# Wider updates of x, odd tiles scaled in PSUM, and a new load order in a hybrid mLSTM/SSD diffusion step

## The chip, the cores and the metric

The kernel runs on one core of a Trainium2 chip. Its time is device time in microseconds (us) of one execution; several runs are taken and the median counts. The engines named below are TensorE (PE; its weight loads are shown apart as PEld), VectorE (DVE), ScalarE (ACT), GpSimd (POOL) and SyncE (SP), which here only issues loads and stores. All data is fp32.

## The reference, cut to what matters

One trunk layer on 128 prompt tokens and 256 latent tokens, D = 2048: a SwiGLU half step, a token mixer, a second SwiGLU half step. Each is fed by a modulated norm and added to x through a second norm and a gate:

```python
mod = (silu(c) @ w_ada + b_ada).reshape(1, 9, D)          # shift, scale, gate for three stages
h = rmsnorm(x, g[0]) * (1 + scale) + shift
x = x + 0.5 * gate * rmsnorm(swiglu(h, w_gate, w_up, w_down), g[1])
h = rmsnorm(x, g[2]) * (1 + scale) + shift                # the same with the mixer's mod
proj = h @ w_in                                           # q, k, v, gates, z, xbc, dt
x = x + gate * rmsnorm(mix, g[3])
h = rmsnorm(x, g[4]) * (1 + scale) + shift
x = x + 0.5 * gate * rmsnorm(swiglu(h, ...), g[5])
```

The mixer runs a chunked mLSTM and a chunked Mamba-2 scan in both directions; its input xbc goes through a depthwise convolution of five taps and its gates through cumulative sums and maxima.

## The kernel before

Every large product is done as three fp32r products: weights and activations are split into a high part (ACT) and a low part (POOL for weights and even tiles, DVE for odd tiles), and PE adds hi x hi, lo x hi and hi x lo (`product`, L804 to L806; in the down projections L921 to L923).

**Pieces and the ring of loads.** A piece is 512 KB of weights in one of eight slots of `w_raw`. SP issues the loads in the order of the pieces (`load`, L700); a load waits until the piece eight places earlier has been used up: a main piece when POOL has made its low part (`make_lo`, L2526, three pieces ahead of PE), a modulation piece (w_ada) when PE has multiplied it (`ada_piece`, L835). PE uses the pieces in the order of the same list.

**Passages.** Between the stages x is updated and normed. There are two passages with a turn of x, after the first FFN and after the mixer, and an end after the second FFN. In `end_of` (L1913) DVE adds the last products to y, finds the root of y's mean square per token block c (0 the prompt, 1 and 2 the latents), and updates x in twelve pieces of 512 columns (`finish`, L1905). ACT squares the same pieces for the next norm (`square_block`, L1443), POOL multiplies y by the gate rows (`gain`, L2537). PE then turns x into 16 tiles of 128 features (`turn`, L885), spreads the roots of x over the partitions (`spread_root`, L896), and DVE scales each turned tile out of PSUM into one of four SBUF tiles (`scaled`, L1759). ACT adds the shift and rounds to the high part (`hi_of`, L1365), POOL (even tiles, L2531) and DVE (odd tiles, `odd_low`, L1773) make the low part. The first products of the next stage follow tile by tile, and each turns a tile four ahead. `HI_ORDER` and `LO_ORDER` say between which tiles ACT and POOL convert the next weight pieces. In `passage` (L1037) PE also runs matmuls of ones whose result nobody reads (`stay_awake`, L880); `WAKE` holds their numbers: 4, 8, 8 in the first passage, 24, 8, 8 in the second.

**The gate stage.** After the first passage PE runs 28 main pieces (gate columns and xbc of w_in) among 28 modulation pieces (the mod of the mixer's gate and some more). Call them m0 to m27 and a0 to a27. The order is a0 to a3, the passage, m0, m1, m2, a4, m3, a5 and so on: a(j) follows m(j-2). The loads have the same order. A group of modulation pieces ends in columns: DVE copies the sums out (`ada_rows_out`, L1796, the copy is L1801), PE turns them into columns (`ada_columns`, L868, the matmul is L876), DVE adds the bias (`ada_store`, L1841). The first group holds a0 to a15, then three groups of four. `MIX_COLUMNS` (L132) says after how many main pieces the columns of a group come. DVE works in order, and between these steps stand the convolutions (`conv`, L2170) and five parts of the gate arithmetic (`gate_part`, L2087). ACT stores the gain rows of the mixer in this stage (`store_gains`, L1437), element by element:

```python
act.dma_start(g_wait[stage, g].rearrange("(k p) -> p k", p=P), coefG[:, :, g], allow_slow_non_contiguous=True)
```

Of the kernel before, what the change touches and what calls it, by code (L numbers as in the profile page):

```python
# [188 lines left out]
WAKE = ((4, 8, 8), (24, 8, 8))  # L189
# [14 lines left out]
XS = [[("x", c, cc) for cc in range(4)] for c in range(3)]  # L204
YS = [("y", c, cc) for c, cc in ADD_ORDER[:6]]
SQUARES = (
    YS + [("y", 0, 2), ("y", 0, 3), ("y", 1, 2)] + XS[0] + [("y", 1, 3), ("y", 2, 2)] + XS[1][:2] + [("y", 2, 3)] + XS[1][2:] + XS[2],
    [("y", c, cc) for cc in (2, 0, 1) for c in range(3)] + [("y", 0, 3)] + XS[0] + [("y", 1, 3)] + XS[1][:2] + [("y", 2, 3)] + XS[1][2:] + XS[2],
    [("y", c, cc) for c, cc in ADD_ORDER],
)  # L210
# [127 lines left out]
def hybrid_step(nc, A):  # L338
    with ExitStack() as ctx:
# [75 lines left out]
        y_square = am(37, 2 * 512).rearrange("p (s n) -> p s n", s=2)  # L415
        y_gain = am(20.5, NCH * 2 * 512).rearrange("p (c b n) -> p c b n", c=NCH, b=2)
# [206 lines left out]
        GAIN_ORDER = [(c, cc) for c in range(NCH) for cc in (1, 2, 3)]  # L623
        GAIN_ORDER = GAIN_ORDER[:5] + [(2, 1)] + [block for block in GAIN_ORDER[5:] if block != (2, 1)]
# [10 lines left out]
        def square_at(stage, name, c, cc):  # L635

            return SQ_BASE[stage] + SQUARES[stage].index((name, c, cc))
# [9 lines left out]
        def wait_finished(eng, stage, c, cc):  # L647

            eng.wait_ge(x_fin, 12 * stage + 4 * c + cc + 1)
# [5 lines left out]
        def tok_block(c, cc):  # L655
            return y_tok[:, c, 512 * cc:512 * cc + 512]

        def x_block(c, cc):
            return x_tok[:, c, 512 * cc:512 * cc + 512]

        def gain_block(c, cc):
            return y_gain[:, c, cc - 2, :] if cc >= 2 else tok_block(c, cc)
# [8 lines left out]
        def g_block(stage, c, cc):  # L671
            return g_rows[stage][:, min(c, 1), 512 * cc:512 * cc + 512]

# [18 lines left out]
        FRESH_FIRST = GATE_FIRST + [FFN2, FFN2 + 1]  # L692
        assert all(p in M_OF for p in FRESH_FIRST)

        with nc.Block() as block:
# [3 lines left out]
            def _(sp):  # L699
# [88 lines left out]
                for n, (c, cc) in enumerate(OUT_BLOCKS):  # L788
                    sp.wait_ge(out_ready, n + 1)
                    dst = A["y_prompt"][0] if c == 0 else A["y_sample"][0, P * (c - 1):P * c]  # L790
                    sp.dma_start(dst[:, 512 * cc:512 * cc + 512], y_tok[:, c, 512 * cc:512 * cc + 512]).then_inc(out_stored, 16)

                sp.wait_ge(out_stored, 16 * NCH * (KT // 4))
# [6 lines left out]
            def _(pe):  # L800
# [79 lines left out]
                def stay_awake(n):  # L880

                    for _ in range(n):
                        pe.matmul(psum[7][:, 0:P], ones[:, :], ones[:, :], start=True, stop=True)

                def turn(stage, k):  # L885
# [151 lines left out]
                def passage(stage):  # L1037

                    stay_awake(WAKE[stage][0])
# [4 lines left out]
                    stay_awake(WAKE[stage][1])  # L1044
# [1701 lines left out]
```

## Time and profile before

| | |
|---|---|
| median of 3 runs | 3092.46 us (3089.41 to 3094.93) |
| profiled execution | 3091.71 us, span 3089.7 us |
| PE busy | 3009.0 us, 97% |
| POOL, DVE, ACT busy | 59%, 43%, 31% |
| DMA | 535.55 MB, mean 173 GB/s |

The span is what the hardware profiler saw between the first and the last instruction; the execution's own time has about 2 us more around it. Matmuls are pipelined, so PE's busy time is not PE at its peak. The granted clock is the share of full speed that PE was given: 1.00 is 2.4 GHz, 0.5 is 1.2 GHz.

### The profile page before, as it was taken

To read this page: it belongs to the slowest core of one execution; us is meant where nothing else is said; L and a number is where in the kernel's file an instruction comes from. 1 tells how busy PE (TensorE), PEld (TensorE's weight loads), DVE (VectorE), ACT (ScalarE), POOL (GpSimd) and SP (SyncE) were. 2 spreads that over 40 slices of the span, in tenths; PEclk is the share of its full clock that TensorE was granted. 3 is DMA by queue.
4 is the path that set the end of the run, shared out by engine and by line. 5 is a ranking of instruction groups with operands and counts; after the bars stand their busy time and mean duration, and the time that the engine had idled before them with its cause. 6 is when DMAs were issued, how large, how long until landed. Compare 5 with 4: busy or idle time off the path is not lost.

```text
span 3089.7 us, 46612 instructions
## 1 busy us (share of the span) xinstructions
PE 3009.0 (97%) x16689; PEld 2769.0 (90%) x16689; DVE 1331.2 (43%) x2849; ACT 971.5 (31%) x1259; POOL 1829.4 (59%) x908
## 2 busy tenths in 40 slices
PE   6999999999999998899999999899999999999998
PEld 2799999999999997789999988899999999999997
DVE  3365566556655665656743353523342111100113
ACT  2322322222223224424432233522222222222223
POOL 2565665565566665537865446566655666666666
PEclk8999999999999999999999999999999999999999
DMA  9866767666566664685444445236554654444343
GB/s 363 280 216 205 226 215 178 209 219 217 192 195 210 218 213 145 213 191 153 143 135 116 127 115 191 78 127 194 166 173 138 147 154 123 128 129 124 127 129 109
DMA packets 472242, 535.55 MB, mean 173 GB/s; under 512 B 37595, under 2 KB 401603, under 8 KB 470723
## 3 DMA queue, kind: packets, MB, share of 16 engines
q1 hardware_dynamic: 427904, 512.82, 53.1%
q10 hardware_dynamic: 44227, 21.30, 2.8%
q8 instruction: 64, 1.05, 0.1%
q14 instruction: 47, 0.39, 0.0%
HBM read 523.31 MB, written 9.69 MB: 173 GB/s over the span
## 4 chain that ended last, share of the span: by engine, by line
PE 77%; POOL 9%; issue 7%; DVE 4%; DMA 2%; ACT 1%; ACTq 1%; POOLq 0%; DVEq 0%; SPq 0%
PE banks L804 17%; PE banks L806 16%; PE banks L805 16%; PE banks L921 8%; PE banks L923 8%; PE banks L922 8%; POOL w_lo L2528 7%; DVE HB L2251 1%; DMA w_raw<-in_w_in_dram 1%; PE banks L835 1%; PE banks L1278 0%; PE banks L1298 0%; ACTq L1490 0%; DMA w_raw<-in_ffn_w_gate_dram 0%; PE banks L1283 0%
## 5 line engine op out<-in xcount | busy, mean ns | idle before, releaser
L2528 POOL TENSOR_TENSOR w_lo<-w_raw,w_hi 128x1024 fp32r<-128x1024 f32 (+1 forms) x668 | 1596.7, 2395 | 1035.0 <-ACT w_hi L1363 1034.5
L804 PE MATMUL banks<-xn_hi,w_hi 128*128 128x384 f32 x3664 | 1248.1, 341 | 13.9 <-POOL w_lo L2528 8.6
L805 PE MATMUL banks<-xn_lo,w_hi 128*128 128x384 f32 x3664 | 1229.0, 335 | 0.0
L806 PE MATMUL banks<-xn_hi,w_lo 128*128 128x384 f32 x3664 | 1228.9, 335 | 0.0
L1363 ACT ACTIVATE w_hi<-w_raw 128x1024 fp32r<-128x1024 f32 (+1 forms) x668 | 704.2, 1056 | 1514.3 <-PE banks L806 668.0
L804 PEld LDWEIGHTS banks<-xn_hi,w_hi 128*128 128x128 f32 x3664 | 691.2, 189 | 43.0 <-issue 26.7
L805 PEld LDWEIGHTS banks<-xn_lo,w_hi 128*128 128x128 f32 x3664 | 691.3, 189 | 4.2 <-issue 2.9
L806 PEld LDWEIGHTS banks<-xn_hi,w_lo 128*128 128x128 f32 x3664 | 691.0, 189 | 0.0
L1820 DVE SCALAR_TENSOR_TENSOR banks<-w_raw,cT,banks 128x256 f32<-128x256 f32 x1372 | 546.0, 482 | 0.0
L921 PE MATMUL banks<-w_hi,hid_hi 128*128 128x512 f32 x1056 | 411.9, 390 | 0.9 <-POOL w_lo L2528 0.9
L923 PE MATMUL banks<-w_lo,hid_hi 128*128 128x512 f32 x1056 | 411.3, 389 | 0.0
L922 PE MATMUL banks<-w_hi,hid_lo 128*128 128x512 f32 x1056 | 411.2, 389 | 0.0
L1974 DVE TENSOR_TENSOR y<-y,banks 128x512 f32<-128x512 f32 x252 | 158.2, 683 | 537.2 <-PE banks L923 537.0
L1985 DVE TENSOR_TENSOR AM<-AM,banks 128x384 f32<-128x384 f32 x88 | 44.8, 551 | 586.1 <-PE banks L806 586.1
L921 PEld LDWEIGHTS banks<-w_hi,hid_hi 128*128 128x128 f32 x1056 | 198.2, 188 | 42.7 <-POOL w_lo L2528 1.4
L923 PEld LDWEIGHTS banks<-w_lo,hid_hi 128*128 128x128 f32 x1056 | 198.2, 188 | 41.4
L922 PEld LDWEIGHTS banks<-w_hi,hid_lo 128*128 128x128 f32 x1056 | 198.2, 188 | 40.5
L2547 POOL TENSOR_TENSOR hid_lo<-AM,hid_hi 128x384 fp32r<-128x384 f32 x88 | 87.7, 1019 | 77.4 <-ACT hid_hi L1393 77.3
L1393 ACT ACTIVATE hid_hi<-AM 128x384 fp32r<-128x384 f32 x88 | 43.5, 525 | 164.9 <-DVE AM L1985 164.9
L2251 DVE SCALAR_TENSOR_TENSOR HB<-HB,AM,maskneg 128x128 f32<-128x128 f32 x96 | 83.3, 935 | 18.0 <-DMA HB<-row_wait 18.0
L835 PE MATMUL banks<-w_raw,cT 128*2 128x256 f32 x736 | 61.1, 432 | 18.1 <-DMA w_raw<-in_w_ada_dram 18.0
L1390 ACT ACTIVATE AM<-banks 128x384 f32<-128x384 f32 x88 | 38.4, 489 | 125.2 <-PE banks L806 125.1
(278 smaller groups left out, 1583.8 us busy)
## 6 DMA issues: line engine op xcount, KB each, us to landing
w_raw<-in_w_ada_dram SPq DMA_DIRECT2D x288, 512.0 KB, 5.6
w_raw<-in_ffn_w_gate_dram SPq DMA_DIRECT2D x176, 512.0 KB, 4.2
w_raw<-in_ffn_w_up_dram SPq DMA_DIRECT2D x176, 512.0 KB, 4.0
w_raw<-in_ffn_w_down_dram SPq DMA_DIRECT2D x176, 512.0 KB, 3.9
w_raw<-in_w_in_dram SPq DMA_DIRECT2D x104, 512.0 KB, 3.8
w_raw<-in_w_out_dram SPq DMA_DIRECT2D x32, 512.0 KB, 3.7
HB<-row_wait ACTq DMA_DIRECT2D x12, 512.0 KB, 4.4
AM<-g_wait SPq DMA_DIRECT2D x4, 1024.0 KB, 9.6
```

The costliest lines, as they stand in the source:

```text
L804: pe.matmul(out, wh, hi, start=start, stop=False)
L805: pe.matmul(out, wh, lo, start=False, stop=False)
L806: return pe.matmul(out, w_lo[:, w, off:off + P], hi, start=False, stop=stop)
L835: last = pe.matmul(ada_bank(unit)[32 * s:32 * s + 2, 0:PC], cT[:, n * q + s // h, :], w_raw[:, p % NR, s * PC:s * PC + PC], start=(q == 0) ...
L921: pe.matmul(bank[:, :], hi, wh, start=start, stop=False)
L922: pe.matmul(bank[:, :], lo, wh, start=False, stop=False)
L923: return pe.matmul(bank[:, :], hi, wl, start=False, stop=stop)
L1363: act.activation(used(w_hi[:, slot(p), :], p), used(w_raw[:, p % NR, :], p), ACT.Copy).then_inc(w_hi_ready, 1)
L1820: ins = dve.scalar_tensor_tensor(out=dst, in0=w, scalar=c, in1=acc, op0=ALU.mult, op1=ALU.add)
L1974: dve.tensor_tensor(tile, tile, psum[token_bank(cc, c)][:, :], ALU.add).then_inc(y_done, 1)
L2251: last = dve.scalar_tensor_tensor(out=seg[:, n % 2, h, :], in0=seg[:, n % 2, h, :], scalar=cols[:, C_Q, c, r0 + h:r0 + h + 1], in1=maskneg ...
L2528: pool.tensor_tensor(used(w_lo[:, slot(p), :], p), used(w_raw[:, p % NR, :], p), used(w_hi[:, slot(p), :], p).bitcast(F32), ALU.subtract). ...
```

## The change

- **Updates of x.** `finish`, `square_block` and the stores of the output take a width. x is updated in seven pieces, (c, first block, blocks): (0,0,2), (0,2,2), (1,0,2), (1,2,2), (2,0,2), (2,2,1), (2,3,1), in a new order of `end_of`. The order of POOL's gains changes with it.
- **Odd tiles.** An odd turned tile is scaled in place in its PSUM bank; ACT and `odd_low` read it there. Odd tiles take turns in two banks, and the turn of tile k waits for the low part of tile k-4.
- **Load order.** The loads of the gate stage get an order of their own: a(j) directly behind m(j), not behind m(j-2). PE's order (now `GATE_ORDER`, `GATE_EXEC`) stays, and counts of PE's events are renumbered to it.
- **Columns.** The first group's columns come after main piece 16 (m15) and not ahead of a16; the others after 21, 25 and 28 main pieces and not 19, 23 and 27.
- **Wake matmuls.** 8 ahead and 4 behind in the first passage, 16 and 4 in the second, none between the roots.
- **Weights between tiles.** In the second passage ACT and POOL convert the sixth and seventh weight piece of the FFN between tiles 12 and 15 and not behind the last tile.

```diff
-MIX_COLUMNS = {19 + 4 * k: ADA_PASS + k for k in range(ADA_MIX)}
+MIX_COLUMNS = {16: 0, 21: ADA_PASS, 25: ADA_PASS + 1, 28: ADA_PASS + 2}
-GATE_PIECES = [("a", 0, q) for q in range(PASS_PIECES)] + GATE_PIECES
+GATE_ORDER = [("a", 0, q) for q in range(PASS_PIECES)] + GATE_PIECES
+GATE_MAINS = [piece for piece in GATE_PIECES if piece[0] == "x"]
+GATE_PIECES = GATE_ORDER[:PASS_PIECES] + GATE_MAINS[:5]
+for k, piece in enumerate(MIX_ADA):
+    GATE_PIECES += [piece] + GATE_MAINS[5 + k:6 + k]
...
+for n, piece in enumerate(GATE_ORDER):
+    N_PE[P_GATES + GATE_PIECES.index(piece)] = N_PE[P_GATES - 1] + n + 1
+GATE_EXEC = [(P_GATES + GATE_PIECES.index(piece), *piece) for piece in GATE_ORDER]
...
-WAKE = ((4, 8, 8), (24, 8, 8))
+WAKE = ((8, 4), (16, 4))
...
+FINISHED = [(0, 0, 2), (0, 2, 2), (1, 0, 2), (1, 2, 2), (2, 0, 2), (2, 2, 1), (2, 3, 1)]
...
-TURN_BANKS = ((1, 4), (4, 6))
+TURN_BANKS = ((4, 1, 5), (4, 6, 7))
...
-            ((2, range(5)), (3, range(5, 8)), (4, range(8, 11)), (None, range(11, KT))))
+            ((2, range(5)), (3, range(5, 8)), (4, range(8, 11)), (5, range(11, 13)), (6, range(13, 15)), (None, (15,))))
...
-            ((1, (0, 2)), (2, (4,)), (3, (6,)), (4, (8, 10)), (None, (12, 14))))
+            ((1, (0, 2)), (2, (4,)), (3, (6,)), (4, (8, 10)), (5, (12,)), (6, (14,))))
...
-        FRESH_FIRST = GATE_FIRST + [FFN2, FFN2 + 1]
+        FRESH_FIRST = GATE_FIRST + [FFN2, FFN2 + 1, FFN2 + 2, FFN2 + 3]
...
                 def turn(stage, k):
-                    if k >= 2:
+                    if k % 2 == 0 and k >= 2:
                         pe.wait_ge(xt_done, KT * (stage + 1) + k - 1)
+                    if k == 3:
+                        pe.wait_ge(xt_done, KT * (stage + 1) + 1)
+                    if k % 2 and k >= 5:
+                        pe.wait_ge(xn_lo_odd, KT // 2 * (stage + 1) + (k - 5) // 2 + 1)
                     for c in range(NCH):
-                        last = pe.transpose(psum[TURN_BANKS[stage][k % 2]][:, P * c:P * c + P], x_tok[:, c, P * k:P * k + P], idn[:, :])
+                        last = pe.transpose(turn_bank(stage, k)[:, P * c:P * c + P], x_tok[:, c, P * k:P * k + P], idn[:, :])
...
                 def passage(stage):
-                    stay_awake(WAKE[stage][0])
+                    stay_awake(WAKE[stage][0], 7)
                     for k in range(2):
                         turn(stage, k)
                     for c in range(2):
                         spread_root(stage, c)
-                    stay_awake(WAKE[stage][1])
                     spread_root(stage, 2)
                     for k in range(2, TURN_AHEAD):
                         turn(stage, k)
-                    stay_awake(WAKE[stage][2])
+                    stay_awake(WAKE[stage][1], 0)
...
                 def scaled(stage, k):
-                    src = psum[TURN_BANKS[stage - 1][k % 2]] if stage else y[:, k, :]
+                    src = turn_bank(stage - 1, k)[:, 0:TOK] if stage else y[:, k, :]
+                    dst = src if stage and k % 2 else xt[:, k % 4, :]
...
                 def odd_low(stage, k):
+                    src = turn_bank(stage - 1, k)[:, 0:TOK] if stage else xt[:, k % 4, :]
...
                 def end_of(stage):
+                    mixer, output = stage == 1, stage == 2
+                    if mixer:
+                        for c in range(NCH):
+                            root_bias(stage, "y", c)
+                    else:
+                        add_last(stage, 0, 2)
+                    add_last(stage, 0, 3)
+                    if not mixer:
+                        root_bias(stage, "y", 0)
+                    inverse(stage, "y", 0)
+                    finish(stage, 0, 0, 2)
+                    if not mixer:
+                        add_last(stage, 1, 2)
+                    finish(stage, 0, 2, 2)
+                    add_last(stage, 1, 3)
+                    if not mixer:
+                        root_bias(stage, "y", 1)
+                    if not output:
+                        root_bias(stage, "x", 0)
+                    inverse(stage, "y", 1)
+                    finish(stage, 1, 0, 2)
+                    if not mixer:
+                        add_last(stage, 2, 2)
+                    finish(stage, 1, 2, 2)
+                    add_last(stage, 2, 3)
+                    if not mixer:
+                        root_bias(stage, "y", 2)
+                    if not output:
+                        root_bias(stage, "x", 1)
+                    inverse(stage, "y", 2)
+                    finish(stage, 2, 0, 2)
+                    if not output:
+                        diagonal(stage, 0)
+                        diagonal(stage, 1)
+                    finish(stage, 2, 2, 1)
+                    finish(stage, 2, 3, 1)
+                    if not output:
+                        root_row(stage, 0, 2)
+                        root_bias(stage, "x", 2)
+                        diagonal(stage, 2)
```

## Rows read from the trace of the kernel before

**Rows 1.** Page, part 1: engine, busy us (share of the span) and instructions.
```profile
PE 3009.0 (97%) x16689; PEld 2769.0 (90%) x16689; DVE 1331.2 (43%) x2849; ACT 971.5 (31%) x1259; POOL 1829.4 (59%) x908
```
**Rows 2.** Windows: start:end, length, then busy us per engine, granted clock, DMA share, GB/s.
```profile
core 0: us, PE busy (x) PEld busy (x) DVE busy (x) ACT busy (x) POOL busy (x), PEclk, DMA share, GB/s
...
1195.00:1260.00 65.00, 51.69 (x311) 43.98 (x310) 44.71 (x93) 38.52 (x97) 34.30 (x25) 0.89 0.35 110
...
1300.00:1360.00 60.00, 49.90 (x301) 43.10 (x300) 41.64 (x79) 13.91 (x20) 18.89 (x8) 0.89 0.74 139
...
1960.00:2000.00 40.00, 32.48 (x208) 30.79 (x207) 25.70 (x59) 26.96 (x58) 21.12 (x14) 0.97 0.17 53
```
**Rows 3.** Timeline of PE, gate stage: start, length, instruction, idle before and releaser.
```profile
1312.18 1.02 PE L876 MATMUL banks<-idn,ada_row 128*128 128x8 f32 x4 [6.52 <-DVE ada_row L1801]
...
1320.27 0.61 PE L835 MATMUL banks<-w_raw,cT 128*2 128x256 f32 x8
...
1325.18 0.61 PE L835 MATMUL banks<-w_raw,cT 128*2 128x256 f32 x8
...
1337.33 0.61 PE L876 MATMUL banks<-sel,ada_row 128*128 128x2 f32 x4 [2.26 <-DVE ada_row L1801]
...
1356.75 0.44 PE L804 MATMUL banks<-xn_hi,w_hi 128*128 128x384 f32 x1 [1.31 <-POOL w_lo L2528]
```
**Rows 4.** Timeline of DVE, gate stage.
```profile
1311.70 0.42 DVE L1801 COPY ada_row<-banks 128x256 f32<-128x256 f32 x1
...
1324.76 3.05 DVE L2188 SCALAR_TENSOR_TENSOR AM<-banks,vecT,AM 128x126 f32<-128x126 f32 x8
...
1336.86 0.42 DVE L1801 COPY ada_row<-banks 128x256 f32<-128x256 f32 x1
```
**Rows 5.** Chain of waits, three pieces: start, length, what.
```profile
1222.22 3.41 PE banks L883 x16
...
1331.18 22.00 DMA w_raw<-in_w_in_dram
...
1966.93 1.79 PE banks L883 x16
```
**Rows 6.** DMA queues from 1330 to 1340: ACT's queue (packets, MB, share).
```profile
q10 hardware_dynamic: 3646, 0.01, 49.6%
```
**Rows 7.** Timeline of ACT's queue: the second store of gain rows.
```profile
1328.33 2.36 ACTq L1441 DMA_DIRECT2D g_wait<-coefG  x1
```
**Rows 8.** Timeline of PE, both passages.
```profile
1219.39 1.54 PE L893 MATMUL banks<-idn,xT 128*128 128x128 f32 x6 [6.89 <-DVE xT L1910]
...
1235.34 0.41 PE L804 MATMUL banks<-xn_hi,w_hi 128*128 128x384 f32 x1 [2.20 <-DVE xn_lo L1778]
...
1973.84 0.41 PE L804 MATMUL banks<-xn_hi,w_hi 128*128 128x384 f32 x1 [0.65 <-DVE xn_lo L1778]
...
1999.10 0.69 PE L804 MATMUL banks<-xn_hi,w_hi 128*128 128x384 f32 x1 [4.50 <-POOL w_lo L2528]
```
**Rows 9.** Windows before and behind PE's waits.
```profile
1209.40:1230.10 20.70, 12.36 (x92) 10.22 (x92) 16.37 (x36) 12.91 (x37) 4.81 (x4) 0.75 0.35 114
...
1235.20:1245.20 10.00, 9.86 (x51) 9.50 (x51) 4.84 (x15) 5.05 (x12) 5.31 (x4) 0.83 0.22 74
1953.00:1968.60 15.60, 12.19 (x101) 11.21 (x100) 14.28 (x32) 10.20 (x30) 4.13 (x3) 1.00 0.11 35
...
1999.10:2004.00 4.90, 4.90 (x15) 4.90 (x16) 0.00 (x0) 0.36 (x1) 4.90 (x3) 0.50 0.62 190
...
1312.20:1318.20 6.00, 6.00 (x25) 5.12 (x26) 0.24 (x2) 0.00 (x0) 0.00 (x0) 0.51 0.48 155
...
1337.40:1342.20 4.80, 4.80 (x25) 4.35 (x26) 0.16 (x1) 1.84 (x6) 0.00 (x0) 0.64 1.18 32
```
**Rows 10.** Two lines of DVE: duration ns min/median/max, first and last start, forms.
```profile
L1769 DVE SCALAR_TENSOR_TENSOR AM<-banks,coefA,AM x64: 335/410/477, 1226.4 to 1993.8; 128x128 f32<-128x128 f32 x32, 128x256 f32<-128x256 f32 x32
...
L1778 DVE SCALAR_TENSOR_TENSOR xn_lo<-AM,modT,xn_hi x48: 335/477/2469, 66.5 to 1996.1; 128x128 fp32r<-128x128 f32 x24, 128x256 fp32r<-128x256 f32 x24
```
**Rows 11.** Timeline of DVE: the last updates.
```profile
3085.72 1.41 DVE L1910 SCALAR_TENSOR_TENSOR y<-AM,norms,xT 128x512 f32<-128x512 f32 x2
```

More of the change, by code:

```diff
@@ L622, in hybrid_step @@
         OUT_BLOCKS = [(c, cc) for c in range(NCH) for cc in range(4)]
-        GAIN_ORDER = [(c, cc) for c in range(NCH) for cc in (1, 2, 3)]
-        GAIN_ORDER = GAIN_ORDER[:5] + [(2, 1)] + [block for block in GAIN_ORDER[5:] if block != (2, 1)]
+        GAIN_ORDER = [(c, 1) for c in range(NCH)] + [(c, cc) for c in range(NCH) for cc in (2, 3)]
         OUT_GAINS = [(c, 2) for c in range(NCH)] + [(c, 1) for c in range(NCH)] + [(c, 3) for c in range(NCH)]
@@ L635, in square_at @@
         def square_at(stage, name, c, cc):
-            return SQ_BASE[stage] + SQUARES[stage].index((name, c, cc))
+            return SQ_BASE[stage] + next(m for m, (x, d, k, w) in enumerate(SQUARES[stage]) if (x, d) == (name, c) and k <= cc < k + w)
         def wait_squared(eng, stage, name, c, cc):
@@ L647, in wait_finished, with tok_block, x_block, gain_block @@
         def wait_finished(eng, stage, c, cc):
-            eng.wait_ge(x_fin, 12 * stage + 4 * c + cc + 1)
+            eng.wait_ge(x_fin, len(FINISHED) * stage + next(m for m, (d, k, w) in enumerate(FINISHED) if d == c and k <= cc < k + w) + 1)
         def last_products(stage, c, cc):
             return (4 * (stage > 0) + 2 * (stage > 1)) + (2 * c + cc - 2 if stage != 1 else c) + 1
[L655 to L662, printed above, removed]
+        def tok_block(c, cc, w=1):
+            return y_tok[:, c, 512 * cc:512 * (cc + w)]
+        def x_block(c, cc, w=1):
+            return x_tok[:, c, 512 * cc:512 * (cc + w)]
+        def gain_block(c, cc, w=1):
+            return y_gain[:, c, 512 * (cc - 2):512 * (cc - 2 + w)] if cc >= 2 else tok_block(c, cc, w)
         def wait_for_gain(eng, stage, c, cc):
@@ L878, in ada_columns, with stay_awake @@
                     last.then_inc(ada_cols, h)
-                def stay_awake(n):
+                def stay_awake(n, bank):
                     for _ in range(n):
-                        pe.matmul(psum[7][:, 0:P], ones[:, :], ones[:, :], start=True, stop=True)
+                        pe.matmul(psum[bank][:, 0:P], ones[:, :], ones[:, :], start=True, stop=True)
                 def turn(stage, k):
@@ L1725, in _ @@
                             mix_high(*of)
-                for name, c, cc in SQUARES[1][9:]:
-                    square_block(1, name, c, cc)
-                    if (name, c, cc) == ("y", 1, 3):
+                for part in SQUARES[1][9:]:
+                    square_block(1, *part)
+                    if part == ("y", 1, 3, 1):
                         make_hi(FFN2)
@@ L1913, in end_of, with finish @@
-                def end_of(stage):
-                    def roots_of_x(c):
-                        if stage < 2:
-                            root_bias(stage, "x", c)
-                    def diagonal_of(c):
-                        if stage < 2:
-                            diagonal(stage, c)
-                    def rows_of(c0, c1):
-                        if stage < 2:
-                            root_row(stage, c0, c1)
-                    last = (3,) if stage == 1 else (2, 3)
-                    for cc in last:
-                        add_last(stage, 0, cc)
-                    root_bias(stage, "y", 0)
-                    if stage != 1:
+                def finish(stage, c, cc, w):
+                    for k in range(max(cc, 1), cc + w):
+                        wait_gained(dve, stage, c, k)
+                    out = tok_block(c, cc, w) if stage == 2 else x_block(c, cc, w)
+                    dve.scalar_tensor_tensor(out=out, in0=gain_block(c, cc, w), scalar=ROOT["y"][:, 1, c:c + 1],
+                                             in1=x_block(c, cc, w), op0=ALU.mult, op1=ALU.add).then_inc(out_ready if stage == 2 else x_fin, 1)
@@ L1932, in end_of @@
                         add_last(stage, 1, 2)
-                    inverse(stage, "y", 0)
-                    for cc in range(4):
-                        finish(stage, 0, cc)
+                    finish(stage, 0, 2, 2)
                     add_last(stage, 1, 3)
-                    root_bias(stage, "y", 1)
-                    roots_of_x(0)
+                    if not mixer:
+                        root_bias(stage, "y", 1)
+                    if not output:
+                        root_bias(stage, "x", 0)
```

108 lines of the change are left out of this document (46 added, 62 removed).

## The prediction

> **What bounds the kernel now.** The first part of the page is read first: TensorE (PE) is busy for 3009.0 of 3089.7 us [rows 1], so the bound is the matmul work of three stages that this change leaves alone, and only the 80.7 us in which PE is idle, and the time it runs at the lower clock, can be won. The view by windows shows where they lie: 13.3 us idle around the first passage, 10.1 in the second half of the gate stage, 7.5 after the second passage, with the granted clock at 0.89, 0.89 and 0.97 there [rows 2]. Most of the rest is in the first 150 us, untouched. In these three windows PE's own timeline and then that of VectorE (DVE) are read for what each wait ended on; the chain of waits tells whether it lay on the path; windows cut around each wait give the clock behind it. The reader is to see that every wait named below is one of PE itself, so a removed microsecond counts unless the next wait takes it back.
>
> **Modulation columns later.** Pieces are counted m0 to m27 (main) and a0 to a27 (modulation). Before, PE wants the first columns ahead of a16 and waits 6.52 us for the row copy L1801 [rows 3], which DVE reaches at 1311.70 behind gate part 2 and ends at 1312.12 [rows 4]. It then runs at clock 0.51 for 6.0 us [rows 9], which loses 0.49 x 6.0 = 2.9. The second columns wait 2.26 [rows 3], and the 4.8 us behind have clock 0.64 [rows 9], 1.7 lost. Then m22 waits 1.31 for its low half [rows 3]. Sum: 6.52 + 2.9 + 2.26 + 1.7 + 1.31 = 14.7. The columns' own matmuls, some 0.5 us each, stay.
>
> A pair of a main and a modulation piece takes 1325.18 - 1320.27 = 4.91 us [rows 3]. The first columns move by one pair: PE asks at 1305.66 + 4.91 = 1310.6 on the old clock, so 1.5 us of the wait is left; what the clock does after so short a wait lies between nothing and 2.9, and I take 1.0. The second move by two pairs, 9.8 us. Their row was ready at 1336.86 + 0.42, 9.6 us after the convolution that ended at 1327.8 [rows 4]; that convolution now starts when m15 ends, or when DVE is free at 1312.1, so the row comes at about 1312.1 + 7.4 + 0.5 + 9.6 = 1329.6, and PE asks at about 1339: no wait. On DVE the first store (L1855) now stands behind the convolution; its reader on PE, a20, comes four pairs later, so 7.4 us more is covered. The last two columns did not wait and do not now.
>
> **Main pieces queued ahead.** The wait of m22 is a DMA: its load was issued at 1331.18 and took 22.00 us [rows 5], because ScalarE's queue had just been given the second of two stores of gain rows in 4-byte elements [rows 7], and for the next 10 us that queue's 3646 packets held 49.6% of the engines for 0.01 MB [rows 6]. The ring has eight slots, and a load waits for the piece eight places earlier. Before, a(j+4) is issued when a(j) has been used, and m(j+3) behind it. After, m(j+5) stands there, so m22 is issued two pairs (9.8 us) earlier against PE, ahead of the store. What is late next is a modulation piece: a23 is still issued when a19 has been used, just behind the store, and PE wants it four pairs and one column later, 4 x 4.91 + 0.5 = 20.1 us. It lands a little under the 22.00 of the load that used to follow it. Its wait is 0 to 2 us; I take 0.7. Left in this stage are 1.5 + 1.0 + 0.7 = 3.2 of 14.7, a gain of 11.5, with bounds 7.5 (2 us of DVE time lost anew to GpSimd, full loss of clock) and 13.5. Early in the stage the piece a9 is now behind m9, which is in flight during the 3 MB spill of x; up to 1 us is in the lower bound.
>
> **Odd tiles in PSUM.** The scaling that reads PSUM (L1769) runs 335 to 477 ns; the odd low half that reads two SBUF tiles (L1778) has the same shortest time, 335, but reaches 2469 [rows 10], when GpSimd works on SBUF at the same time. With one operand in PSUM it should behave as L1769 does. The waits that this makes on PE are 2.20 us in the first passage and 0.65 in the second [rows 8]. The first is followed by 10.0 us at clock 0.83 [rows 9], 1.7 lost. Gain: 3.9 and 0.65; the low end is 2.2 and 0, if the clock falls anyway and the low half now waits for ScalarE. The turn of an odd tile now waits for the low half four tiles back, which the products need first, so I cost it at nothing; without that cover it is one such operation pair, 0.8 us. The Trainium skill (VectorE: DVE Perf Modes, the section on the TRN2 errata) gives an instruction that reads PSUM a fixed cost of 120 cycles where one from SBUF has 58, at 0.96 GHz 65 ns more. By it the 32 low halves would cost 2.1 us of DVE time as an estimate; the equal minima of [rows 10] show no such surcharge.
>
> **Wide updates and their order.** Twelve updates of 512 columns become seven, of squares on ScalarE likewise. DVE's bytes are the same, so what goes is a fixed cost per instruction and the order: the first inverse no longer stands behind an addition that waits for PE, and two diagonals stand behind the update that PE's first turn wants. Before, PE is idle 6.89 us until that update in the first passage [rows 8]. The same DVE work in a new order, with new collisions with GpSimd, may give nothing or 3.1 us; I take 1.5, and in the second passage, where PE's turn waits less, 0.5 of 0 to 1.0. At the end of the kernel the last update ends at 3085.72 + 1.41 = 3087.1 [rows 11] and the store follows; I take 0.3, between 1.2 and a loss of 0.5. SP issues seven stores for twelve; the last is still one of 512 columns, so nothing is saved behind the last update.
>
> **Fewer wake matmuls.** The middle ones are on the chain in the first passage for 3.41 us [rows 5]: the third root waits behind them. But the diagonal that feeds it is not ready at their start; I take 1.6 of 0 to 3.4. The last ones are on the chain for 1.79 in the second passage [rows 5]; half go: 0.4 in the first and 0.3 in the second, each between 0 and 0.9. Against this stands the clock. With 24 + 8 + 8 it was 1.00 up to the first product of the second passage, with 4 + 8 + 8 it was 0.75 in the first [rows 9]. With 16 + 4 and 8 + 4 PE does little between, and I expect the first products at 1.2 GHz: a loss between 0 and the 2.9 worked out above, 1.6 in the first and 1.2 in the second passage. The Trainium skill (TensorE: Matmul & The Clock Gate, What's actually happening) has the low clock as the default state, released by activity only; the 0.51 after the idle 6.52 us agrees. By it both starts pay in full, rival C.
>
> **Weights between the tiles.** After the second passage PE waits 4.50 us for the low half of the sixth weight piece [rows 8], made only after all tiles, and then runs at clock 0.50 for 4.9 us [rows 9], 2.45 lost. Now it is made after tile 12. Three tiles of ScalarE's work no longer stand ahead of it; I leave 0.5 and gain 6.4, between 4.5 and 6.95. Tile 13 and those behind come one weight conversion later on ScalarE; the products of a whole piece (4.91 less 0.6 for the modulation piece [rows 3]) cover that. On GpSimd the low half of tile 14 now stands behind this conversion and is wanted after the same piece.
>
> **The sum.** First passage 1.5 + 1.6 + 0.4 + 3.9 - 1.6 = 5.8. Gate stage 11.5. Second passage 0.5 + 0.3 + 0.65 + 6.4 - 1.2 = 6.65. End 0.3. Together 24.2. The profiled execution took 3091.71 us (2.0 around its span), 0.75 under the median of the runs: 3091.7 - 24.2 = 3067.5, as a median 3068.2.
>
> **The rivals.**
> A, the forecast: 3068, its own range 3062 to 3074.
> B, the wait turns from main to modulation pieces: the tiny-element store still lasts as long, a23 waits in full and the row copy slips behind GpSimd, so that the gate stage gives 11.5 - 1.3 (a23) - 1.9 (clock) - 2 (DVE) = 6.3: 5.2 us less than A, 3073.4. For it: the ring still has four modulation slots, and their lead in pairs is unchanged. Against: only one is issued into the store's time and wanted before it ends.
> C, the clock: both passages start cold at the full 2.9, and the remaining wakes at half clock add 1 us each: 5 us less, 3073. For it: 0.75 in [rows 9]. B and C together: 3079.
> D, slower: a(j) now queues behind m(j), whose slot comes free only when GpSimd has converted m(j-4); ScalarE, which feeds GpSimd, sits five times behind a convolution (3.05 us for the taps of one half [rows 4], 7.4 for both). If each such block held a modulation piece up for its whole length, 5 x 7.4 = 37 us would be lost against 24 won: 3105. It decides from the point where a piece lands over 4 x 4.91 = 19.6 us after its forerunner is used. Against: only loads under the store came near that.
> E, no change: DVE's row copies move along with the columns and the passages only trade wakes for a cold clock: 3091.
>
> **How the numbers follow.** A 0.58, B 0.16, C 0.14, B with C 0.05, D 0.03, E 0.04. The time is A's. The range 3058 to 3080 holds A with its bounds, B, C and both, and leaves out D and E. Its low end is about the sum of all best ends: 11.3 + 13.5 + 9.5 + 1.2 = 35.5, or 3057. Two runs of this kernel tell no change from 0.2%, 6.2 us: faster 0.92, same 0.04, slower 0.04.
>
> **What would show it.** Right: PE's wait on L1801 falls to 1 to 3 us at the first and to nothing at the second columns; no L804 waits for L1778; the sixth weight piece waits under 1 us; L1778 stays under 500 ns in the passages. Wrong: PE's L835 waiting for w_ada loads over 2 us (B), windows at the first products with a clock of 0.5 for over 5 us (C), or repeated L835 waits through the whole gate stage (D).

## The result and the profile after

The changed kernel takes 3065.03 us (median of four runs, 3064.63 to 3065.42) against 3092.55 for the kernel before. The ratio is 0.9912 with a 95% interval of 0.9894 to 0.9929. The profiled execution has a span of 3063.5 us, 26.2 less than before. PE's idle time fell from 80.7 to 62.0 us and its busy time by 7.5 [rows 1]. Of the 7.5, 6.7 are wakes (the six groups of L883 took 16.2 us before, the four of L896 take 9.5), so 0.8 us are left for the clock, better in one place and worse in another:

```profile
PE 3001.5 (98%) x16633; PEld 2761.7 (90%) x16633; DVE 1314.5 (43%) x2830; ACT 967.9 (32%) x1239; POOL 1832.1 (60%) x908
```

By windows the three stages look like this (columns as in [rows 2]; the third window is 19 us earlier, as the stage is):

```profile
1195.00:1260.00 65.00, 56.49 (x347) 46.99 (x346) 38.63 (x87) 37.77 (x88) 40.55 (x27) 0.92 0.47 155
1300.00:1360.00 60.00, 58.33 (x379) 51.24 (x378) 40.04 (x94) 19.32 (x26) 26.56 (x12) 0.97 0.82 194
1941.00:1981.00 40.00, 36.33 (x209) 35.06 (x208) 19.80 (x57) 26.03 (x56) 24.10 (x15) 0.87 0.23 71
```

The first two gained in idle time and in clock; the third has half its idle time (3.7 for 7.5 us) but a lower clock, 0.87 for 0.97. PE's timeline gives the places. Line numbers have shifted: L817 is the product that was L804, L848 the modulation piece L835, L889 the columns L876, L910 the turn L893, L916 the spread of the roots, L896 the wakes L883; L1932 is the update of x that was L1910, L1925 the diagonal L1903, L1818 the row copy L1801, L1785 the scaling L1769, L1795 the odd low half L1778, L2544 GpSimd's low half of the weights L2528. In the experiments they shift again by up to four lines.

```profile
1209.22 1.91 PE L848 MATMUL banks<-w_raw,cT 128*2 128x256 f32 x32
...
1214.71 0.87 PE L910 MATMUL banks<-idn,xT 128*128 128x128 f32 x6 [1.60 <-DVE xT L1932]
...
1219.32 0.80 PE L916 MATMUL banks<-AM,ones 128*128 128x128 f32 x2 [2.50 <-DVE AM L1925]
...
1224.55 0.42 PE L817 MATMUL banks<-xn_hi,w_hi 128*128 128x384 f32 x1
...
1227.21 0.52 PE L910 MATMUL banks<-idn,xT 128*128 128x128 f32 x3 [0.20 <-DVE xn_lo L1795]
...
1248.38 0.69 PE L817 MATMUL banks<-xn_hi,w_hi 128*128 128x384 f32 x1 [2.20 <-POOL w_lo L2544]
...
1304.22 0.61 PE L889 MATMUL banks<-idn,ada_row 128*128 128x8 f32 x4 [1.67 <-DVE ada_row L1818]
1304.77 0.61 PE L848 MATMUL banks<-w_raw,cT 128*2 128x256 f32 x8
...
1311.27 0.61 PE L848 MATMUL banks<-w_raw,cT 128*2 128x256 f32 x8
...
1331.46 0.50 PE L889 MATMUL banks<-sel,ada_row 128*128 128x2 f32 x4
...
1940.37 0.98 PE L910 MATMUL banks<-idn,xT 128*128 128x128 f32 x6 [2.09 <-DVE xT L1932]
...
1944.14 0.80 PE L916 MATMUL banks<-AM,ones 128*128 128x128 f32 x2 [1.94 <-DVE AM L1925]
...
1949.70 0.67 PE L817 MATMUL banks<-xn_hi,w_hi 128*128 128x384 f32 x1
...
1975.77 0.45 PE L817 MATMUL banks<-xn_hi,w_hi 128*128 128x384 f32 x1 [0.48 <-POOL w_lo L2544]
```

Against [rows 3, 8]: the first columns wait 1.67 us instead of 6.52, the second not at all; no product waits for w_lo in the second half of the gate stage; the 6.89 us ahead of the first turn are 1.60; the 2.20 and 0.65 us that a product waited for an odd low half are gone, but three turns wait some 0.2 us each for one (the first at 1227.21); the sixth weight piece waits 0.48 instead of 4.50. One long wait of a product stayed, that of the main piece m5 (2.20 us at 1248.38). The same instructions' starts in three traces, cut into stretches:

| stretch (us) | before | changed | changed, second execution (e9) | forecast of change |
|---|---|---|---|---|
| start of the first passage | 1209.50 | 1209.22 | 1208.19 | 0 |
| to its first product | 20.83 | 15.33 | 15.66 | -3.5, clock apart |
| to a4 | 14.95 | 11.60 | 12.48 | -3.9 and clock |
| a4 to a7 | 16.91 | 18.02 | 18.18 | 0 |
| a7 to a15 | 38.50 | 38.50 | 38.48 | 0 |
| a15 to a27 | 76.17 | 64.76 | 63.53 | -11.5 |
| to the second passage | 576.25 | 577.12 | 576.01 | 0 |
| to its first product | 15.69 | 15.15 | 15.17 | -0.8, clock +1.2 |
| to the first down product | 95.11 | 88.58 | 88.64 | -7.05 |
| to the end of the span | 1025.79 | 1025.22 | 1025.26 | -0.3 |

The clock behind the waits, by windows (the column behind POOL's):

```profile
1219.30:1224.50 5.20, 3.93 (x18) 3.67 (x19) 3.73 (x11) 3.57 (x10) 1.01 (x1) 0.53 0.00 0
...
1248.30:1253.00 4.70, 4.62 (x18) 4.62 (x19) 1.05 (x2) 1.88 (x2) 4.70 (x5) 0.66 1.03 418
...
1304.20:1310.20 6.00, 5.98 (x31) 5.52 (x32) 5.75 (x15) 0.52 (x1) 1.96 (x1) 0.72 0.55 178
...
1940.40:1946.20 5.80, 2.61 (x13) 2.05 (x13) 4.25 (x14) 3.84 (x9) 0.00 (x0) 0.55 0.00 0
```

The second passage, at 1.00 before [rows 9], is now cold.

### The profile page after: what moved, and what is told of

Same layout as the page of the kernel before. It is cut to its first block, busy times and chain, and to the rows that moved or that the text cites. A ratio compares the mean times of both kernels' runs of the same rounds, so it can differ in the third digit from the quotient of the medians.

```text
span 3063.5 us, 46459 instructions
## 1 busy us (share of the span) xinstructions
PE 3001.5 (98%) x16633; PEld 2761.7 (90%) x16633; DVE 1314.5 (43%) x2830; ACT 967.9 (32%) x1239; POOL 1832.1 (60%) x908
## 4 chain that ended last, share of the span: by engine, by line
PE 79%; POOL 9%; issue 7%; DVE 3%; DMA 1%; ACT 1%; ACTq 1%; POOLq 0%; DVEq 0%
PE banks L817 17%; PE banks L819 17%; PE banks L818 17%; PE banks L938 8%; PE banks L939 8%; PE banks L940 8%; POOL w_lo L2544 7%; DVE HB L2267 1%; PE banks L848 1%; PE banks L1207 0%; PE banks L1292 0%; PE banks L1312 0%; DMA w_raw<-in_ffn_w_gate_dram 0%; ACTq L1505 0%; PE banks L1297 0%
## 5 line engine op out<-in xcount | busy, mean ns | idle before, releaser
L2544 POOL TENSOR_TENSOR w_lo<-w_raw,w_hi 128x1024 fp32r<-128x1024 f32 (+1 forms) x668 | 1596.3, 2395 | 1011.3 <-ACT w_hi L1377 1008.5
L817 PE MATMUL banks<-xn_hi,w_hi 128*128 128x384 f32 x3664 | 1247.5, 340 | 5.2 <-POOL w_lo L2544 2.7
L817 PEld LDWEIGHTS banks<-xn_hi,w_hi 128*128 128x128 f32 x3664 | 690.8, 189 | 33.3 <-issue 26.5
L848 PE MATMUL banks<-w_raw,cT 128*2 128x256 f32 x736 | 61.3, 431 | 17.5 <-DMA w_raw<-in_w_ada_dram 17.5
```

The lines of the kernel that those rows point to most:

```text
L817: pe.matmul(out, wh, hi, start=start, stop=False)
L848: last = pe.matmul(ada_bank(unit)[32 * s:32 * s + 2, 0:PC], cT[:, n * q + s // h, :], w_raw[:, p % NR, s * PC:s * PC + PC], start=(q == 0) ...
L2544: pool.tensor_tensor(used(w_lo[:, slot(p), :], p), used(w_raw[:, p % NR, :], p), used(w_hi[:, slot(p), :], p).bitcast(F32), ALU.subtract). ...
```

## The experiments

The runs were taken in groups, each with the kernel before beside them; its median was 3092.55 us beside the changed kernel and 3091.80, 3089.97 and 3089.54 beside e1 to e4, e5 to e8 and e9 to e12. Where two runs are compared across groups, it is by their ratio to that median (0.001 is 3.1 us); stretches of the table above are compared directly. A ratio's interval reaches some 4 to 5 us to either side, and only those of e2 and e8 lie clear of the changed kernel's. The differences of the others are carried by the waits and stretches of one profiled execution each, and by e9 to e12 being one group.

**e1: the old order of loads.**

```
-GATE_PIECES = GATE_ORDER[:PASS_PIECES] + GATE_MAINS[:5]
-for k, piece in enumerate(MIX_ADA): ...
+GATE_PIECES = list(GATE_ORDER)
```

> The changed kernel with the loads issued in the old order, each modulation piece directly behind the main piece two places on; everything else as changed. Theory: the columns' move alone does not keep the loads behind the store of gain rows off the path. A main piece issued right behind that store (at about a18) lands some 20 us later and is wanted, with the conversions of 3.5 us, some 20.5 us later: a wait of 1.3 to 3.5 us for w_lo at m21 or m22 and up to 2 us at the low clock behind it, 3067 to 3071 us. Rival: with the columns out of the way the old order is just as good, 3064.5 to 3065.5, and no wait for w_lo over 0.5 us in the second half of the gate stage.

3070.46 us, ratio 0.9931 (0.9918 to 0.9945). PE's waits in the second half of the gate stage:

```profile
1337.18 0.61 PE L846 MATMUL banks<-w_raw,cT 128*2 128x256 f32 x8 [1.01 <-DMA w_raw<-in_w_ada_dram]
1342.08 0.69 PE L815 MATMUL banks<-xn_hi,w_hi 128*128 128x384 f32 x1 [4.29 <-POOL w_lo L2542]
```

A main piece waits again, and longer than before (4.29 for 1.31): its load takes 22.0 us as before [rows 5], but PE, no longer held up at the columns, wants it 21.2 us after its issue and not 24.3. The theory holds, its wait was set too low.

**e2: the columns at their old places, new order of loads.**

```
-MIX_COLUMNS = {16: 0, 21: ADA_PASS, 25: ADA_PASS + 1, 28: ADA_PASS + 2}
+MIX_COLUMNS = {19 + 4 * k: ADA_PASS + k for k in range(ADA_MIX)}
     (and the first columns and their store ahead of a16 again)
```

> The changed kernel with the modulation columns at their old places (first ahead of a16, the next four main pieces apart from 19) and the new load order. Theory: the columns' move is nearly all of the gate stage's gain: waits of about 6.5 and 2.3 us on the row copy come back with a low clock behind them, against 1.67 and 1.6 lost now: 10 to 11 us more, 3074 to 3076, and no wait at m22 since its load stays ahead of the store. Rival: a good part came from the loads, and DVE, which is freer now, has the row earlier: 3067 to 3070.

3075.42 us, 0.9945 (0.9932 to 0.9959).

```profile
1303.78 1.02 PE L889 MATMUL banks<-idn,ada_row 128*128 128x8 f32 x4 [6.51 <-DVE ada_row L1820]
...
1328.54 0.61 PE L889 MATMUL banks<-sel,ada_row 128*128 128x2 f32 x4 [2.10 <-DVE ada_row L1820]
...
1351.69 0.61 PE L889 MATMUL banks<-sel,ada_row 128*128 128x2 f32 x4 [0.68 <-DVE ada_row L1820]
```

The old waits are back, with a new one of 0.68, and no main piece waits; the theory holds. From a15 to a27 it takes 75.31 us, e1 70.09, before 76.17. Beside the second execution of the changed kernel, whose clock, like e1's, held behind the first columns (63.53), undoing the columns costs 11.8 and undoing the loads 6.6, but undoing both, as in the kernel before, only 12.6: with the columns in their old places the loads' order is worth 0.9 us, with the new places 6.6. The two edits belong together. Each of these stretches is of one execution, and of e1's 6.6 some 0.7 is a23's wait, which differs from execution to execution.

**e3: odd tiles scaled into SBUF.**

```
-dst = src if stage and k % 2 else xt[:, k % 4, :]
+dst = xt[:, k % 4, :]      (the readers in L1384 and L1793 likewise)
```

> The changed kernel with the scaled odd tiles written to SBUF again and read there by ScalarE and by the low half; the banks and waits of the turns stay. Theory: the low halves collide with GpSimd again, single ones reach 1 to 2.5 us, and PE waits for them in the first passage: 2 to 4.5 us more, 3067 to 3069.5. Rival: the new order of VectorE and the wakes moved the low halves away from GpSimd's instructions, and the bank they read does not matter: 3064.5 to 3066.

3066.57 us, 0.9917 (0.9904 to 0.9931): 1.5 us more by the ratios, inside the noise and between the theory's range and the rival's. The waits decide, and two of them are the theory's; the one between, for a modulation piece, is no matter of the tiles:

```profile
1227.66 0.52 PE L910 MATMUL banks<-idn,xT 128*128 128x128 f32 x3 [1.82 <-DVE xn_lo L1795]
...
1336.63 0.61 PE L848 MATMUL banks<-w_raw,cT 128*2 128x256 f32 x8 [2.21 <-DMA w_raw<-in_w_ada_dram]
...
1955.29 0.52 PE L910 MATMUL banks<-idn,xT 128*128 128x128 f32 x3 [1.77 <-DVE xn_lo L1795]
```

The low half's durations (ns, min/median/max) in the two kernels, first changed, then e3, show why:

```profile
L1795 DVE SCALAR_TENSOR_TENSOR xn_lo<-banks,modT,xn_hi x32: 339/412/477, 1223.6 to 1976.9; 128x128 fp32r<-128x128 f32 x16, 128x256 fp32r<-128x256 f32 x16
```

```profile
L1795 DVE SCALAR_TENSOR_TENSOR xn_lo<-AM,modT,xn_hi x48: 340/481/2616, 65.1 to 1980.6; 128x128 fp32r<-128x128 f32 x24, 128x256 fp32r<-128x256 f32 x24
```

And the collision behind the wait at 1227.66, GpSimd's timeline and VectorE's of e3:

```profile
1223.84 2.39 POOL L2544 TENSOR_TENSOR w_lo<-w_raw,w_hi 128x1024 fp32r<-128x1024 f32 x1
1226.19 1.05 POOL L2551 TENSOR_TENSOR xn_lo<-AM,xn_hi 128x384 fp32r<-128x384 f32 x1
```

```profile
1225.17 2.34 DVE L1795 SCALAR_TENSOR_TENSOR xn_lo<-AM,modT,xn_hi 128x128 fp32r<-128x128 f32 x2
```

The two low halves, 0.73 us in the changed kernel, end only when both of GpSimd's instructions have. The stretches to a4 (13.49) and to the down products (91.14) are 1.0 and 2.5 us longer than in the second execution of the changed kernel (1.9 and 2.6 against the first). Less of it shows in the time, in the profiled execution because the clock held behind m5 (7.28 us from a6 to a7, where the changed kernel has 8.60 and 8.77) and the first passage began at 1207.43, 0.8 to 1.8 us earlier. The Trainium skill (SBUF — State Buffer, Who interferes with whom) says that a VectorE instruction with two SBUF inputs contends with a GpSimd instruction that reads SBUF, and one with at most one SBUF input does not; these rows agree.

**e4: the weight pieces of the second passage in their old order.**

```
-(4, range(8, 11)), (5, range(11, 13)), (6, range(13, 15)), (None, (15,))
+(4, range(8, 11)), (None, range(11, KT))      (GpSimd's order likewise)
```

> The changed kernel with the weight pieces of the second passage converted in the old order, the sixth and seventh only after all tiles. Theory: the wait of some 4.5 us for the sixth piece and the low clock behind it (2.45) come back: 5.5 to 7 us more, 3070.5 to 3072. Rival: the earlier passage and the shorter low halves leave ScalarE and GpSimd time, and the wait shrinks to 1 or 2 us with half the clock loss: 3066.5 to 3068.5.

3070.43 us, 0.9931 (0.9918 to 0.9945).

```profile
1978.35 0.69 PE L817 MATMUL banks<-xn_hi,w_hi 128*128 128x384 f32 x1 [3.92 <-POOL w_lo L2544]
...
1978.30:1983.30 5.00, 4.96 (x15) 4.96 (x16) 0.00 (x0) 0.40 (x1) 5.00 (x3) 0.50 0.63 195
```

The stretch to the down products is 94.15 us, 5.5 more: 3.92 - 0.48 of waiting; the rest fits the clock, which is 0.50 for the next 5.0 us. The theory holds.

**e5: more wakes.**

```
-WAKE = ((8, 4), (16, 4))
+WAKE = ((14, 4), (24, 8))      and stay_awake(8, 7) ahead of spread_root(stage, 2)
```

> The changed kernel with more wake matmuls: 14 and 24 at the start of the two passages (8 and 16 as changed), 8 again ahead of the third spread of the roots, 4 and 8 last. Theory: in the second passage the fewer wakes cost a cold clock (0.55 and 0.50 up to the first product), worth some 1.5 us there and a few tenths in the first passage; with them back the clock is 1.00 from the last feed-forward matmul to the first product and the time is 3062.5 to 3064. The wakes themselves cost nothing, since PE waits 1.6 to 2.5 us for VectorE at those places. Rival: the middle wakes stand in front of the third root as they did before, 1 to 2 us each passage, which eats the clock's gain: 3064.5 to 3067.

3060.95 us, 0.9905 (0.9890 to 0.9920): 2 us less than the changed kernel by the ratios, as the theory has it, though inside the noise. In both passages the clock is full; the second:

```profile
1937.80:1943.30 5.50, 3.58 (x29) 3.23 (x29) 4.26 (x14) 3.85 (x9) 0.00 (x0) 1.00 0.00 0
```

The second passage reaches its first product in 14.07 us (15.17 in the second execution of the changed kernel) and the down products in 87.83 (88.64): the cold clock cost 1.9 us there. In the other executions with wakes of 16 and 4 and the second passage as changed the two sum to 1.0 to 2.1 us more than here. The first passage reaches its first product 1.1 to 1.4 us sooner and a4 0.3 to 1.5, since two products now wait for GpSimd (0.31 and 0.46 us). The middle wakes, on the chain for 3.41 us at the low clock before [rows 5], now fit into PE's wait for the third root, of which 0.7 us is left.

**e6: each wide update as two instructions.**

```
-dve.scalar_tensor_tensor(out=out, in0=gain_block(c, cc, w), ...)
+for k in range(w): last = dve.scalar_tensor_tensor(out=out[:, 512 * k:512 * k + 512], ...)
```

> The changed kernel with each wide update of x done as two instructions of 512 columns in the same place of the new order (squares and stores stay wide). Theory: the gain of the first passage comes from the order on VectorE, not from the width: two of 512 take what one of 1024 does to within 0.1 us, so 3064.5 to 3066. Rival: the width itself saves fixed time and collisions with GpSimd: 1 to 2 us in the first passage and as much at the end, 3067 to 3069.

3066.78 us, 0.9926 (0.9913 to 0.9940): 4 us more by the ratios. One update on VectorE, first in the changed kernel, then in e6:

```profile
1209.93 1.28 DVE L1932 SCALAR_TENSOR_TENSOR xT<-AM,norms,xT 128x1024 f32<-128x1024 f32 x1
```

```profile
1209.10 2.43 DVE L1933 SCALAR_TENSOR_TENSOR xT<-AM,norms,xT 128x512 f32<-128x512 f32 x2
```

Undisturbed, two narrow ones take 1.41 or 1.42 us, 0.14 more than a wide one; here the second got behind a GpSimd instruction. The first turn starts 7.53 us into the passage, against 5.49 in the changed kernel and 9.89 before, and the end of the kernel is 1.8 us longer (1027.04). The theory, order alone, falls: of the 4.4 us ahead of the first turn, 2.0 are the width's. The other 2.4 are put down to the new order by subtraction; the wide squares and GpSimd's new order of gains are in it too, and no run takes these apart.

**e7: two waits that the change left.**

```
-GATE_AT = {3: 0, 5: 1, 9: 2, 12: 3, 17: 4}
+GATE_AT = {3: 0, 5: 1, 10: 2, 12: 3, 17: 4}
-(4, range(8, 11)), (5, range(11, 14)), (None, range(14, KT))
+(4, range(8, 11)), (5, (11,)), (None, range(12, KT))      (GpSimd's order likewise)
```

> Two waits that the changed kernel has left. The weight piece m5 of the first passage is converted after tile 11 instead of after tile 13, and gate part 2 stands on VectorE one main piece later, behind the row copy of a15. Theory: both waits (2.20 on w_lo and 1.67 on the row copy) go with the low clock behind them (about 1.6 each): 5 to 7 us less, 3058 to 3060. Rival: VectorE is full there, so the later gate part makes a convolution late and PE waits for that instead, and only m5 gains: 3061 to 3063.

3057.65 us, 0.9893 (0.9878 to 0.9908): 5.9 us less. From a6 to a7 it takes 4.93 us (8.60), from a15 to a17 10.15 (12.10), and neither wait is in the timeline; no convolution is late. A modulation piece (a24) waits 0.55 us. The theory holds.

**e8: the store of gain rows behind the gate stage.**

```
-if (n, q) == (3, 1): store_gains(1)
 conv_silus(XBC_T // 2 - 1)
+store_gains(1)
```

> The changed kernel with the second store of gain rows (4-byte elements) issued behind the last convolution of the gate stage instead of in the middle of it. Theory: in the changed kernel the loads behind that store land so close to their use that a modulation piece (a23) waits 0 to 2.2 us, differently in each execution; without it 0 to 1 us less, 3063.5 to 3065, no wait for a modulation piece, and nothing lost later, where eight pieces of one kind are ahead in the ring. Rival: the store takes 10 us or more of the DMA engines wherever it stands, and the mixer's loads wait instead: 3066 to 3068.

3075.46 us, 0.9951 (0.9937 to 0.9964): 12 us more. The theory falls; the rival had the kind of loss, a load of the mixer, but not its size.

```profile
1402.05 1.97 PE L1191 MATMUL banks<-idn,xT 128*128 128x128 f32 x8 [12.51 <-DMA xT<-in_state_ssm_dram]
```

PE waits for the load of the scan's state, which stands on the store's own queue. The queues from 1374 to 1384 (packets, MB, share), and the issues there (count, KB each, us to landing):

```profile
q10 hardware_dynamic: 1759, 0.10, 72.3%
...
w_raw<-in_w_in_dram SPq DMA_DIRECT2D x3, 512.0 KB, 18.2
xT<-in_state_ssm_dram ACTq DMA_DIRECT2D x2, 512.0 KB, 20.7
```

The same issues in the changed kernel:

```profile
w_raw<-in_w_in_dram SPq DMA_DIRECT2D x3, 512.0 KB, 3.7
xT<-in_state_ssm_dram ACTq DMA_DIRECT2D x2, 512.0 KB, 6.1
```

In those 10 us ScalarE's queue moved 0.10 MB and SP's nothing. SP's weight loads land late too (18.2 us), but PE does not wait for them there. The Trainium skill (DMA: Bandwidth & Descriptors, Queues, rings and completion order) has ScalarE's queue as one ring on each of the DMA engines, consumed in ring order. These rows do not show that order by itself, since loads on the other queue landed nearly as late.

**e9: the changed kernel again.** No edit.

> The changed kernel itself once more, as a yardstick beside the next three and for a second look at three things that differ from execution to execution: the start of the first passage (1206.7 to 1210.4 us so far), the clock behind the 1.67 us wait for the first columns (the pair behind it took 6.50 us in the changed kernel, 4.91 in four others with the same wait), and the wait of a modulation piece behind the store of gain rows (0 to 2.2 us). Theory: these are properties of the execution, not of the edits: 3064.5 to 3066.5, first columns wait 1.67 again, the pair behind them 4.9 or 6.5, the modulation piece 0 to 2.2. Rival: they belong to the kernel and come out the same as before: 6.50 and 0.

3062.96 us, 0.9911 (0.9895 to 0.9928): by the ratio the same as at first, though the time lies under the range expected, in a group where the kernel before is 3.0 us faster as well. The same wait, another clock behind it:

```profile
1304.54 0.61 PE L889 MATMUL banks<-idn,ada_row 128*128 128x8 f32 x4 [1.67 <-DVE ada_row L1818]
```

```profile
1304.50:1309.90 5.40, 5.36 (x36) 4.74 (x36) 5.19 (x14) 0.53 (x1) 1.98 (x1) 1.00 0.56 187
```

The pair behind it took 4.91 us, not 6.50. The modulation piece a23 waited 0.27 us, where it did not wait in the first execution. The theory holds.

**e10: no wakes.** WAKE = ((0, 0), (0, 0)).

> The changed kernel without any wake matmul in the two passages. Theory: PE, idle for longer, does the turns, the spread of the roots and the first products at 1.2 GHz: 1 to 2 us more in the second passage than with 16 and 4 and 0.5 to 1.5 more in the first, 3066.5 to 3069. Rival: with 8 + 4 and 16 + 4 the passages are cold already, so that fewer change nothing, and without the last ones the first product comes some tenths earlier: 3064 to 3065.5.

3061.96 us, 0.9912 (0.9895 to 0.9928): no difference from the changed kernel by the ratios; the rival holds. Both passages are cold, as this window of the second shows,

```profile
1937.40:1943.60 6.20, 3.20 (x13) 2.64 (x13) 4.36 (x15) 3.88 (x9) 0.00 (x0) 0.50 0.00 0
```

but the first products come 1.1 and 0.8 us sooner, because the last wakes (1.8 to 1.9 us at the low clock) no longer stand ahead of them. Part of the profiled execution's time is chance: its clock held behind m5 (7.19 us from a6 to a7).

**e11: e5 and e7 together.**

> The two edits that shortened the changed kernel, together: m5 after tile 11 with gate part 2 one main piece later, and wakes of 14, 8, 4 and 24, 8, 8. Theory: they lie in different stretches and add up: 7 us from the first and 2 to 2.5 from the second, 3054.5 to 3056.5. Rival: with the first product 1 us earlier GpSimd is late with the low halves of tiles and weights in the first passage, waits of 0.3 to 0.8 us, and half of the wakes' gain goes there: 3056.5 to 3058.

3056.25 us (3053.16 to 3058.43), 0.9887 (0.9871 to 0.9904). By the ratios 7.7 us are gained, where e5 and e7 had 2.2 and 5.9: they add up, as in the first passage's stretches (14.21 us to the first product, 4.92 from a6 to a7). The rival's waits for GpSimd are there (0.31 and 0.47 us), but e5 had them already. In the profiled execution the clock was 0.61 ahead of the second passage's first products and its stretch took 15.69 us, 1.6 more than in e5 and e12 with the same wakes; that may be a part of the spread.

**e12: the store in two parts.**

```
-if (n, q) == (3, 1): store_gains(1)
+if (n, q) in ((2, 1), (3, 1)): store_gains(1, (n - 2,))      on top of e11
```

> As the run before, with the two stores of gain rows issued four main pieces apart, one at the old place and one four main pieces before it. Theory: each holds the engines for half as long, and no modulation piece waits any more: 0 to 1 us less than the run before, 3054 to 3056. Rival: the time that loads take behind such a store hangs on its queue's number of packets in all, and a piece waits behind each of the two: 0.5 to 2 us more.

3055.58 us (3055.44 to 3055.85), 0.9889 (0.9872 to 0.9905), the fastest median of all: 7.4 us less than the changed kernel and 34 less than the one before, in the same group. No modulation piece waits, where e11's a24 waited 0.60, and no load behind either part takes more than 13.8 us to land, where e11's took up to 21.1. Against e11 the median says nothing; the runs lie closer.

## Why the prediction was right

The forecast was 3068.2, the measurement 3065.0, and the profiled spans differ by 26.2 where the sum was 24.2. Two things in that difference belong to no edit: the first passage's start (1206.7 to 1210.4 us over all these executions) and the stretch from a27 to the second passage (576.0 to 577.8, e8 apart), together 0.6 us to the changed kernel's loss. The four signs that the prediction named for being right are all there: 1.67 us at the first columns and nothing at the second, no product waiting for an odd low half, 0.48 us at the sixth weight piece, low halves of 477 ns at most in the passages. That the sum comes within 2 us is in part luck: by stretches 4.3 us too little, 2.9 of them on VectorE, stand against 2.3 us of terms that gave less or were not forecast.

*Gate stage, 11.5 forecast, 11.4 measured (12.6 in the second execution).* The three terms left over were 1.5 of waiting, 1.0 of clock and 0.7 for a23; they came out as 1.67, 1.59 or 0, and 0 or 0.3. (The 9.6 us between convolution and row are 9.5 by [rows 4]; nothing hangs on it.) e2 shows the columns as the main part and e1 the loads as what keeps it. What the working by single losses did not show is that the loads' order was worth more than the 1.31 us at m22: the wait that it removes would have grown to 4.29.

*First passage, 5.8 forecast, 8.9 (7.6) up to a4.* VectorE's part is the term that was mis-sized: "nothing or 3.1 us; I take 1.5". The first turn came 4.4 us sooner into the passage, above the upper bound. "DVE's bytes are the same, so what goes is a fixed cost per instruction and the order" left out that each instruction is also a place where GpSimd can get in ahead; e6 puts 2.0 us of the 4.4 on the width: some 0.7 for five pairs at 0.14 us, as an estimate, and the rest for such places. The odd low halves went by the mechanism worked out, with equal minima in PSUM and SBUF (339 and 340 ns), but gave less than the 3.9: from the first product to a4 3.4 us (2.5 in the second execution) came off, and three turns wait 0.6 us together for the low half that was costed at nothing. e3 gives back 1.0 to 1.9 of it here and 2.5 in the second passage, where 0.65 was forecast: the collisions fall elsewhere in the new order. The Trainium skill's surcharge (VectorE: DVE Perf Modes, TRN2 errata) does not show in those minima. The wakes and the clock, -1.6 - 0.4 + 1.6, came to -1.1 (-0.8) from the first turn to the first product.

*Not forecast: m5.* Its wait shrank from 2.77 to 2.20, but the clock fell behind it, to 0.66, so that a4 to a7 grew by 1.1 us.

*Second passage, 6.65 forecast, 7.1 measured.* Up to the first product 0.8 was to be gained and the cold clock to cost 1.2. The first turn came 0.7 us sooner (5.82 us into the passage for 6.56) and the wakes ahead of the third root went, so 0.5 us were left over although the clock cost more than forecast (1.0 to 2.1 for 1.2, by e5). The sixth weight piece gave what was worked out; e4 returns 5.5 of the 6.4.

*End, 0.3 forecast, 0.6 measured*; e6, 1.8 us longer there, shows that it hangs on the width.

*The rivals.* B: a modulation piece does wait in six of the thirteen executions since the change, 0.27 to 2.21 us, never in a row. C: half true; its sign is there, 0.53 and 0.55 over 5.2 and 5.8 us up to the first products, yet the cost stays inside the forecast's own terms. D: no repeated waits on modulation pieces. E is excluded by the interval.

## What to carry to other kernels

When two edits remove waits on one engine, take each out of the pair and look at the stretch, not at the wait: an engine that runs ahead meets the next late transfer sooner, so a repair of loads can be worth five times the wait that the old trace shows (6.6 for 1.31 us here). Count instructions on VectorE not only by their bytes but by how often each must get past GpSimd; one wide instruction has fewer such places, and with an operand in PSUM none showed here. The wakes paid only where they filled PE's wait to its end, and not in every execution even then (e11's second passage); a few that left the clock low only stood in the way.

## What the runs showed of the hardware

The clock behind a short wait is not fixed by the wait. Nine executions had the same 1.66 to 1.68 us ahead of the first columns; in seven the pair behind it took 4.91 to 4.94 us, in two (the changed kernel, e5) 6.50 and 6.49. Behind the 2.2 us at m5, two of ten kept the clock (7.28 and 7.19 us from a6 to a7), eight did not (8.60 to 8.77). The Trainium skill (TensorE: Matmul & The Clock Gate, What's actually happening) says that the same kernel, at its start, warms up after different numbers of matmuls from run to run. These stretches show the like in the middle of a kernel, and 1 to 3 us of a time such as this, as an estimate from the 1.6 us at either wait, are no property of the kernel.

A store of two rows of 8 KB in 4-byte elements makes the 512 KB loads issued behind it land late on either queue: on the other queue after up to 22.0 us before, 20.0 in the changed kernel, 18.3 in e8 and 23.1 in e3, on its own after 19.8 and 21.6 in e8, where the weight loads of the whole profile have medians of 3.7 to 5.8. With the two rows four main pieces apart (e12) it is 13.8 at most.
